# A two-layer mixer block on one core: block sums of the MLP input taken from f32 columns, one tile slot apart, with the residual scaled on GpSimd and its bias added on VectorE

## The reference

```python
# first layer
u2 = _layer_norm(x) * (1.0 + scale2[:, None, :]) + shift2[:, None, :]
f = jnp.square(jax.nn.relu(u2 @ w_ff1[l])) @ w_ff2[l]
x = _layer_norm(DEEPNORM_ALPHA * x + gate2[:, None, :] * f, ln2_w[l], ln2_b[l])

# second layer
def squared_relu_mlp(x, w1, w2):
    hdn = jnp.square(jax.nn.relu(jnp.einsum('bld,df->blf', x, w1.astype(jnp.float32))))
    return jnp.einsum('blf,fd->bld', hdn, w2.astype(jnp.float32))

h = layer_norm(ALPHA * h + squared_relu_mlp(h, mlp_w1[l], mlp_w2[l]), ln3_g[l], ln3_b[l])
```

## Time and profile before

| what | value |
| --- | --- |
| median of 3 runs | 2819.01 us (2818.23 to 2820.32) |
| the profiled execution | 2814.59 us |
| its span, first to last instruction | 2812.8 us |
| mean granted TensorE clock | 0.969 |
| busy: TensorE, VectorE, ScalarE, GpSimd | 92%, 56%, 38%, 30% |
| chain that ended last | TensorE 71%, VectorE 13% |

### The profile page before, as it was taken

How to read it: one execution, slowest core, us unless ns; L and a number is a source line. 1 busy time by engine, 2 the same in 40 slices (tenths; PEclk the granted TensorE clock), 3 DMA queues, 4 the chain that set the end, 5 groups by cost and what they waited for, 6 DMA issues and landing times.

```text
span 2812.8 us, 33556 instructions
## 1 busy us (share of the span) xinstructions
PE 2601.7 (92%) x13052; PEld 1338.5 (48%) x13052; DVE 1574.0 (56%) x2452; ACT 1066.2 (38%) x1318; POOL 838.4 (30%) x429
## 2 busy tenths in 40 slices
PE   6999999887899999999988899888999789999998
PEld 3677766433344444444464444344544234444443
DVE  6255344566755565565675749654336764444445
ACT  3434315025344334334244353253424334344441
POOL 1212024012244344441542231126013523333232
PEclk9999999999999999999989999999999899999999
DMA  7311131201012222221021230110001011111121
GB/s 308 117 53 68 43 120 48 88 30 34 30 60 72 72 72 72 83 69 41 31 90 68 68 116 30 45 45 30 31 30 60 30 45 46 60 45 46 60 76 60
DMA packets 71167, 182.50 MB, mean 65 GB/s; under 512 B 6080, under 2 KB 12640, under 8 KB 64224
## 3 DMA queue, kind: packets, MB, share of 16 engines
q1 hardware_dynamic: 55328, 138.89, 14.5%
q10 hardware_dynamic: 15680, 41.46, 4.3%
HBM read 170.90 MB, written 9.45 MB: 64 GB/s over the span
## 4 chain that ended last, share of the span: by engine, by line
PE 71%; DVE 13%; ACT 5%; DVEq 4%; issue 2%; ACTq 2%; POOLq 1%; DMA 1%; POOL 0%; SPq 0%
PE PS L773 21%; PE PS L774 21%; PE PS L775 21%; DVE XT L2344 1%; PE PS L812 1%; DVE Hf L2344 1%; ACT WB L1626 1%; PE PS L1559 1%; DVEq L2343 1%; ACT WS L1628 1%; ACTq L1884 1%; PE PS L1532 1%; PE PS L1061 1%; POOLq L699 1%; DVE Hf L2342 1%
## 5 line engine op out<-in xcount | busy, mean ns | idle before, releaser
L773 PE MATMUL PS<-WB,Hf 128*128 128x512 f16 x1440 | 552.4, 384 | 36.5 <-DVE R L2700 22.1
L618 POOL TENSOR_TENSOR WB<-WS,WB 128x512 f16<-128x512 f32 x208 | 256.7, 1268 | 1012.9 <-ACT WS L1628 1012.9
L774 PE MATMUL PS<-WB,Hf 128*128 128x512 f16 x1440 | 551.4, 383 | 0.0
L775 PE MATMUL PS<-WB,Hf 128*128 128x512 f16 x1440 | 550.8, 383 | 0.0
L773 PE MATMUL PS<-XT,WB 128*128 128x512 f16 x1088 | 420.0, 386 | 43.4 <-DVE Hf L2342 38.2
L774 PE MATMUL PS<-XT,WB 128*128 128x512 f16 x1088 | 419.0, 385 | 0.0
L775 PE MATMUL PS<-XT,WB 128*128 128x512 f16 x1088 | 418.7, 385 | 0.0
L2700 DVE SCALAR_TENSOR_TENSOR R<-PS,R 128x512 f32<-128x512 f32 x320 | 220.5, 691 | 261.8 <-PE PS L775 243.8
L641 POOL TENSOR_TENSOR WB<-WS,WB 128x1024 f16<-128x1024 f32 x84 | 188.8, 2248 | 435.2 <-ACT WS L1927 233.1
L773 PEld LDWEIGHTS PS<-WB,Hf 128*128 128x128 f16 x1440 | 142.2, 99 | 219.0 <-DVE R L2700 25.8
L1626 ACT ACTIVATE WB<-WS 128x2048 f16<-128x2048 f32 (+3 forms) x94 | 167.3, 1779 | 161.8 <-PE PS L775 130.7
(11 more groups left out here) (405 smaller groups left out, 3963.7 us busy)
## 6 DMA issues: line engine op xcount, KB each, us to landing
WS<-in_w_ff SPq DMA_DIRECT2D x32, 1024.0 KB, 5.1
WS<-in_mlp_w SPq DMA_DIRECT2D x32, 1024.0 KB, 5.2
WS<-in_w_mix SPq DMA_DIRECT2D x20, 1024.0 KB, 4.8
Hf<-in_w_ada ACTq DMA_DIRECT2D x12, 1024.0 KB, 5.8
Hf<-in_w_ada SPq DMA_DIRECT2D x8, 1024.0 KB, 10.6
WS<-in_w_out SPq DMA_DIRECT2D x8, 1024.0 KB, 5.0
R<-in_x SPq DMA_DIRECT2D x4, 1024.0 KB, 9.3
R<-in_x ACTq DMA_DIRECT2D x2, 2048.0 KB, 7.8
```

What stands on the lines that cost most here:

```text
L618: op = pool.tensor_tensor(WB[:, slot, 1, at:at + n], WS[:, hf, i * n:(i + 1) * n], WB[:, slot, 0, at:at + n], ALU.subtract)
L773: pe.matmul(o, ah, bh, start=(first and k == 0), stop=False, skip_group_check=True)
L774: pe.matmul(o, ah, bl, start=False, stop=False, skip_group_check=True)
L775: mm = pe.matmul(o, al, bh, start=False, stop=(last and k == n - 1), skip_group_check=True)
```

## The change

- ScalarE writes the scaled input columns of the blocks to f32 tiles in S instead of `TMP`: for mlp1 the left half of the sequence (a11, a12), for mlp2 all four blocks. `split_piece` reads them there and makes the f16 pair as before; the tiles lie where the f16 sums of the same k go later. The joins of these blocks fall away: mlp1 has two per k, mlp2 none.
- The corner work of a k takes three job slots, from job 4 to job 15. In mlp1: joins and `s1`, then `s3`, `s2`, `s4`, then four remainders, with ScalarE's four casts after the third slot's job. In mlp2: all four sums, nothing, four remainders, with the casts in the second slot. Nothing of it is left in the down product.
- ScalarE rounds the halves of the chunk of block 1 before jobs 3 and 5 and those of the down chunk of block 0 before jobs 9 and 12.
- In mlp2 GpSimd only multiplies the residual rows, counted by the new semaphore `res_scaled`. VectorE waits for row tile t before each accumulation on it, and adds the bias, 512 columns at a time, after each accumulation of the down product of block 1.

```diff
+        KEPT_BLOCK = {"a11": "s3", "a12": "s4", "a21": "s1", "a22": "s2"}
+        def sum_tile(m, name, k):
+            return unit(S, SIGN_UNITS[m][name][0], 2)[:, k * HALF:(k + 1) * HALF]
...
+        def block_tile(m, hf, k):
+            if m is None or (m == "mlp1" and hf == 1):
+                return None
+            return sum_tile(m, KEPT_BLOCK["a%d%d" % (hf + 1, k // 4 + 1)], k % 4)
...
+        CAST_SLOT = {"mlp1": 2, "mlp2": 1}
+        def sum_source(m, name):
+            return kept(m, *{"s1": (1, 1), "s3": (1, 0), "s2": (0, 0), "s4": (0, 1)}[name])
...
                     if m == "mlp2":
-                        residual(2, "wo", 0)
-                    else:
+                        pool.wait_ge(ln_rows, 3)
+                        need_side_done(pool, SIDE["wo"] + 15)
+                        pool.wait_ge(piece_done, PIECES["wo"])
+                        for t in range(TT):
+                            pool.tensor_tensor(R[:, t, :], R[:, t, :], S[:, 0, :], ALU.mult)
+                            pool.drain().then_inc(res_scaled, 1)
+                    if m == "mlp1":
...
+                    tile = block_tile(m, hf, k)
+                    if tile is None:
+                        to_tmp(PS[:, b, :], ACT.Identity, scale(k), bias(k)).then_inc(tmp_full, 1)
+                    else:
+                        Q[0] += 1
+                        act.activation(tile, PS[:, b, :], ACT.Identity, scale=scale(k), bias=bias(k)
+                                       ).then_inc(tmp_full, 1)
...
+                def corner_casts(slot):
+                    k = slot // 3
+                    if slot < 0 or slot % 3 != CAST_SLOT[m]:
+                        return
+                    act.wait_ge(corner_sum, 16 * (m == "mlp2") + 4 * k + 4)
+                    for name in ("s1", "s3", "s2", "s4"):
+                        act.activation(sum_rows(m, name, 0, k), sum_source(m, name), ACT.Copy).then_inc(corner_hi, 1)
+                def hidden(u, setup=None):
                     for i in range(8):
-                        if first and i == 4:
-                            round_chunk(c0 + 1)
+                        if u == 0 and i in (3, 5):
+                            round_part(c0 + 1, i // 4)
+                        if u == 1 and i in (1, 4):
+                            round_down(0, i // 4)
...
-                        if corners is not None and i >= corners:
-                            for n in ((), (0, 1), (2,), (3,))[i % 4]:
-                                corner_cast((i - corners) // 4 + (corners == 0), n)
+                        corner_casts(8 * u + i - 4)
...
-                    if u == fast[0]:
-                        corner_cast(3, 2)
-                        corner_cast(3, 3)
...
-                        for hf in range(2):
-                            round_down(u - 1, hf)
-                        hidden(corners=0 if fast and u == 1 else None)
+                        hidden(u)
...
+                def corner_joins(k):
+                    for name, dst in (("a21", kept(m, 1, 0)), ("a22", kept(m, 1, 1))):
                         dve.tensor_tensor(dst, block_rows(name, 0, k), block_rows(name, 1, k), ALU.add)
+                def corner_sums_of(k, names):
+                    a11, a12 = sum_tile(m, "s3", k), sum_tile(m, "s4", k)
+                    a21, a22 = ((sum_tile(m, "s1", k), sum_tile(m, "s2", k)) if last else
+                                (kept(m, 1, 0), kept(m, 1, 1)))
...
+                def corners(slot):
+                    k, i = slot // 3, slot % 3
+                    if slot < 0:
+                        return
+                    if i == 0 and last:
+                        corner_sums_of(k, ("s1", "s3", "s2", "s4"))
+                    if i == 0 and not last:
+                        corner_joins(k)
+                        corner_sums_of(k, ("s1",))
+                    if i == 1 and not last:
+                        corner_sums_of(k, ("s3", "s2", "s4"))
                     if i == 2:
+                        corner_remainders(k)
...
+                        if last and between is not None:
+                            dve.wait_ge(res_scaled, t + 1)
...
-                    if u == 1 and last:
-                        dve.wait_ge(res_ready, 24)
                     def between(j):
+                        if last and u == 2:
+                            r = R[:, j % 8, (j // 8) * HALF:(j // 8 + 1) * HALF]
+                            dve.drain()
+                            op = dve.tensor_tensor(r, r, S[:, 1, (j // 8) * HALF:(j // 8 + 1) * HALF], ALU.add)
+                            if j >= 8:
+                                op.then_inc(res_ready, 1)
```

More of the change, by code:

```diff
@@ L462, in program @@
         ln_rows = sem("ln_rows")
-        res_ready = sem("res_ready")
+        res_ready, res_scaled = sem("res_ready"), sem("res_scaled")
         kv_ready = sem("kv_ready")
@@ L1836, in load_rows, with norm_tail @@
                 act.dma_start(S[:, at + 1, :], bias.to_broadcast([P, D])).then_inc(par_in[name], 16)
-            def norm_tail(roots, scale, bias, first, early=False, second=True):
+            def norm_tail(roots, scale, bias, first, early=False, second=True, m=None):
                 if early:
@@ L1848, in norm_tail @@
                     if t == 3:
-                        columns_half(scale, bias)
-                columns_half(scale, bias)
+                        columns_half(scale, bias, m, 0)
+                columns_half(scale, bias, m, 1)
                 if second:
@@ L1858, in _ @@
             norm_tail(2, lambda k: MODC[:, 3, k:k + 1], lambda k: MODC[:, 2, k:k + 1], C["mlp1"],
-                      second=False)
+                      second=False, m="mlp1")
             def mlp(m, name, lnw, lnb, last):
@@ L2028, in s5_setup @@
                             act.dma_start(S5_LAMBDA[k].rearrange("(j p) -> p j", p=P), q(n), allow_slow_non_contiguous=True).then_inc(lambda_out, 16)
-                hidden(None if last else s5_setup, first=True, corners=4 if fast else None)
+                hidden(0, None if last else s5_setup)
                 for u in range(1, NF):
                     if u in fast:
-                        if u == fast[0]:
-                            corner_cast(3, 0)
-                            corner_cast(3, 1)
                         up_forms(u)
@@ L2313, in _ @@
             norm_tail(1, lambda k: col("ln2_g_2", k), lambda k: col("ln2_b_2", k), C["mlp2"],
-                      second=False)
+                      second=False, m="mlp2")
             mlp("mlp2", "ln3_2", I["ln3_g_2"], I["ln3_b_2"], True)
@@ L2737, in _ @@
                 if t == 3:
-                    columns_half(0, XT)
-            columns_half(1, XT)
+                    columns_half(0, XT, "mlp1")
+            columns_half(1, XT, "mlp1")
             J[0] += 2 * TT
@@ L2876, in mlp, with setup @@
                             split_hidden(u, n)
-                    elif u < 2:
-                        hidden(u, (first_corners, next_corners)[u])
+                    else:
+                        def setup(j):
+                            if u == 0 and not last:
+                                s5_setup(j)
+                            corners(8 * u + j - 4)
+                        hidden(u, setup)
                     if u == 0:
                         continue
-                    if u == 1 and last:
-                        dve.wait_ge(res_ready, 24)
                     def between(j):
+                        if last and u == 2:
[4 more added lines that the diff above has]
+                                op.then_inc(res_ready, 1)
                         if u in fast and j in (1, 2):
                             split_hidden(u, 5 + j)
-                        if fast and u == 1:
-                            for n in {0: (36, 37, 38), 1: (39, 40, 41), 4: (42, 43), 5: (44, 45), 8: (46, 47)}.get(j, ()):
-                                corner_step(n)
                         if u + 1 in fast:
@@ L3344, in _ @@
             J[0] = WIDE["wo"]
-            out_rows("ln2_2", O_SCALE)
+            out_rows("ln2_2", O_SCALE, "mlp2")
             mlp("mlp2", None, "ln3_2", True)
```

95 lines of the change are left out of this document (26 added, 69 removed).

## The result

| what | before | with the change |
| --- | --- | --- |
| median | 2818.62 us, 4 runs (2816.96 to 2820.32) | 2772.55 us, 4 runs (2771.47 to 2775.43) |
| profiled execution, its span | 2814.59, 2812.8 us | 2772.66, 2770.9 us |
| mlp1 stretch (103.6 us of matmuls) | 133.5 us | 113.0 us |
| mlp2 stretch (113.9 us) | 150.7 us | 126.4 us |
| mean granted clock | 0.969 | 0.971 |

The change is **1.6% faster**, clear of the noise: ratio 0.9838, 95% interval 0.9821 to 0.9855, 46.1 us between the medians. The forecast was 2779 in a range of 2761 to 2797; the likeliest case is the one that came.

What follows compares the result with a forecast made beforehand. TensorE and its waits for VectorE were taken to bound the kernel. Savings of 19.3 us in mlp1 and 20.8 in mlp2, 40.1 us, gave 2774.5 from 2814.6; with 4.4 to the median, 2779 us, range 2761 to 2797.

Steps and rivals of the forecast that it cites:

- The account of the excess: Stretches of mlp1 and mlp2 exceed TensorE's full-clock matmul time by 29.9 and 36.8 us, from waits for VectorE and clock.
- S5 wait: In mlp1, the S5 setup on VectorE between the casts of jobs 4 and 5 keeps TensorE waiting 6.1 us.
- mlp1, what stays: Of mlp1's excess 10.6 us stay (setup wait, its clock, half clock at the start) and 19.3 go.
- Rounding a half at a time: In mlp1, two pairs of ScalarE roundings instead of four in a row remove a 9.2 us wait and 2 us of half clock.
- 9.9 us, it fits: ScalarE's jobs, casts and one pair of roundings take 9.9 us, within the 15.5 us of three jobs, where GpSimd rests.
- mlp2, what stays: Of mlp2's excess 16 us stay (lateness at job 13, its clock, pieces around the first down jobs) and 20.8 go.
- The bias: 16 additions on VectorE inside mlp2's down product of block 1 cost 0, since VectorE has idle time there.
- rival (c): Bias additions in mlp2 wait behind GpSimd and cost 7 us: 2786 us, chance 0.04.
- (b): Casts waiting for full sets of four sums hold ScalarE; mlp2 keeps 30 of 36.8 us: 2793 us, chance 0.14.
- (d): Gain absorbed: the weights' way sets the first quadrant product of block 2 whatever comes before: 2819 us, chance 0.04.
- (e): Slower: many short waits leave the clock at 1.2 GHz in mlp2's block 1 and down product: 2862 us, chance 0.04.
- (a): All but the start goes: S5 setup clears in time, banks swallow mlp2's backlog, 60 us saved: 2759 us, chance 0.16.

Runs made afterwards that it cites:

- no_bias: The changed kernel without the 16 bias additions of mlp2, left out of the computation: 2771.75 us, ratio 0.9840.
- no_scaling: The changed kernel without GpSimd's eight multiplications of the residual in mlp2, left out of the computation: 2759.40 us, ratio 0.9786.
- small_pieces: The changed kernel with GpSimd's gate multiplications, first down chunk split and residual multiplications cut into pieces of 512 elements: 2768.75 us, ratio 0.9821.

## Why the prediction was right, and where it was not

- **The account of the excess held.** One S5 wait in mlp1, one wait of 4 to 6 us in block 1 of mlp2, the bias free, all by the steps named. Expected were stretches of 114 and 130 us; they are 113.0 and 126.4.
- **mlp1, what stays: 10.6 us forecast, 9.4 measured**, of the same three parts: wait 5.2 (6.1 in the forecast), its clock 2.35 (2.4), the slow start 1.7 (2.1). (Waits are taken here from start to start of the matmuls, 0.15 us above the profile's; the wait before is 6.2 that way.) The wait was expected to stay since GpSimd's multiplications follow its split wherever that lies, and so they did (670.28 and 675.11).
- **"Rounding a half at a time" was the wrong name for mlp1's 9.2 us.** The term was 9.2 + 2 us. Alone the edit is worth 0.8, behind the new corner work 5.3; the corner work alone brings 15.2 where it was put at 8.0. The prediction read the earlier trace rows, four roundings in a row, as if ScalarE were punctual otherwise. It was late already: job 8 was done by 676.6, the roundings began at 697.4, 21 us later, and the job was taken at 704.6. What had held ScalarE were casts that waited for sums: the earlier trace rows have 34.9 us of idle time ahead of six casts, 20.9 of them ahead of the first, while VectorE had the S5 setup and its first corner steps. The sum of the two terms came out at 19.3 for 20.5 because the second gave what the first lacked; that they made up for each other was luck.
- **"9.9 us, it fits" compared each engine's busy time with 15.5 us.** VectorE's and ScalarE's shares of three jobs lie largely one behind the other (sums, casts, roundings, job, cast, remainders), and in mlp2 that chain takes 17.9 us. It holds 2.8 us of a cast behind GpSimd's split, too: "it fits where GpSimd rests" left out that each pair of roundings brings a split with it. In mlp1, where the casts stand a slot later, ScalarE's sets come 14.0, 14.0 and 10.3 us apart (687.09, 701.08, 715.08, 725.39), and its down product has no wait. That the place of the casts makes this difference is argued from the two timelines; no run moved it.
- **mlp2, what stays: 16 us forecast, 12.5 measured.** The wait at job 13 is 4.7 us (5.5 in the forecast), its clock 1.3 (2), the pieces at the down jobs 6.3 (8.5); here place and cause were right, and only the sizes a little high. The multiplications took 21.2 us (21.6), VectorE's remainders beside them 2.7 to 2.8 (2.7).
- **The bias and rival (c).** The price of 0 was right, by no_bias. The rule of the Trainium skill's page SBUF — State Buffer, section Who interferes with whom, held as such: of 14 additions in the piece, eleven took 0.69 us and the three that came while GpSimd worked 1.6 (mean 888 ns). VectorE's idle time ahead of the accumulations fell from 17.1 us to 3.3. But that idle time was there to be used, and nobody waited.

```profile
L2895 DVE TENSOR_TENSOR R<-R,S 128x512 f32<-128x512 f32 x14 | 12.4, 888 | 1.6 <-issue 0.4
L2718 DVE SCALAR_TENSOR_TENSOR R<-PS,R 128x512 f32<-128x512 f32 x14 | 9.7, 692 | 3.3 <-issue 1.3 <-PE PS L797 1.3
```

- **The 6.4 us between forecast and median**: the forecast took 4.7 us too little from the stretches (44.8 came, not 40.1). Against that stand 2.9 us lost outside them, which the sum did not have and whose cause stays open. The last 4.5 us come from adding the distance between the profiled execution before and its median (4.4 us). That was a trait of that one execution: after the change the two lie 0.1 us apart.
- **The rivals.** (b) did not come: ScalarE does wait for full sets, 13.7 and 8.6 us, but mlp2 keeps 12.5 us and not 30. (d) and (e) are out by the stretches and by granted clocks of 0.95 and 0.99. (a) did not come: the S5 wait stayed, and the banks hold mlp2 only without the multiplications (no_scaling).

## What to carry to other kernels

When two engines hand work to each other within a stage, add up the chain of hand-overs and compare that with the pace of the engine they feed; the busy time of each says little, and a lateness from elsewhere is only made up if the chain is shorter than the pace. Before a wait is priced as the gain of an edit, ask whether the engine that releases it was already late for another reason: then the edit pays only behind the other one, and the two are measured with four kernels (neither edit, each alone, both). Where VectorE and GpSimd take turns, move GpSimd's large operations to where VectorE has idle time, and look at what they push away: here each move uncovered the next limit within 5 us.

## What was not expected of the hardware

- When both have operations queued that the other blocks, VectorE and GpSimd take turns, one operation each, and this costs GpSimd by the number of its operations: one of 1024 elements takes 2.35 to 2.58 us beside VectorE's, two of 512 take 2.7 to 3.2. Halved pieces so cost GpSimd 3.9 us over the eight rows, and lower VectorE's price from 2.83 us to 1.6 and 1.75, a little more than half.
- A wait of 2.6 us ahead of the second down job in small_pieces was followed by matmuls 0.40 us apart, the lower clock level, and 24 matmuls took 6.9 us instead of 5.2. In the down product of mlp1 before, waits of up to 3.0 us left the clock at 1.00. In that of mlp2, the same kernel, the same wait of 3.01 us was followed by the lower level: the granted clock was 0.58 from 2276.8 to 2280.8. So the length of a wait of some 3 us does not tell what the clock will do after it, and the prediction's argument against (e), drawn from mlp1 alone, was weaker than it looked.

```profile
2202.39 0.38 PE L808 MATMUL PS<-WB,Hf 128*128 128x512 f16 x1
2205.40 0.61 PE L806 MATMUL PS<-WB,Hf 128*128 128x512 f16 x1 [2.63 <-DVE Hf L2370]
2205.80 0.63 PE L807 MATMUL PS<-WB,Hf 128*128 128x512 f16 x1
```

The wait of 3.01 us in the kernel before, in mlp1 and in mlp2:

```profile
763.15 0.39 PE L773 MATMUL PS<-WB,Hf 128*128 128x512 f16 x1 [3.01 <-DVE R L2700]
763.37 0.38 PE L774 MATMUL PS<-WB,Hf 128*128 128x512 f16 x1
763.59 0.38 PE L775 MATMUL PS<-WB,Hf 128*128 128x512 f16 x1
```

```profile
2276.82 0.39 PE L773 MATMUL PS<-WB,Hf 128*128 128x512 f16 x1 [3.01 <-DVE R L2700]
...
2277.54 0.63 PE L773 MATMUL PS<-WB,Hf 128*128 128x512 f16 x1
2277.97 0.63 PE L774 MATMUL PS<-WB,Hf 128*128 128x512 f16 x1
```
